# Queries and keys transposed once instead of doubled, in a one-core attention and recurrence kernel

## The chip, the cores and the metric

The kernel runs on one core of a Trainium2 chip. The metric is the device time in microseconds of one launch, as the median of several runs. Shorter is better.

## What is computed

One layer of a hybrid encoder for a prompt of 2048 frames and a running stream of 64 frames with 128 cached ones. The model width is 1024. There are four attention heads (two maps with a query and key width of 64, values of 128) and four recurrent heads with a 128x128 state. Cut to what matters:

```python
qa, ka, va, za, qr, fr, ir, zr = _project(_rmsnorm(h, norm_g), w_in)
q = qa.reshape(b, s, ATTN_HEADS, 2, ATTN_HEAD_DIM)       # two maps of 64
k = ka.reshape(b, s, ATTN_HEADS, 2, ATTN_HEAD_DIM)
scores = einsum('bqhmd,bkhmd->bhmqk', q, k) * ATTN_SCALE + bias   # -inf where not visible
p = softmax(scores)
a = p[:, :, 0] - lam * p[:, :, 1]
oa = einsum('bhqk,bkhe->bqhe', a, v)
h_new, orec = _rec_scan(silu(qr), key(fr), log_f(fr), ir)   # chunkwise, 64 frames
y = _rmsnorm(h + concat(_rmsnorm(oa) * silu(za), _rmsnorm(orec) * silu(zr)) @ w_out, final_g)
```

The outputs are y, the new keys and values, and the recurrent states, for the prompt and for the sample.

## The kernel before, in words

**Tiles and stages.** The rows are cut into 17 tiles of 128 rows: t=0 to 15 are the prompt, t=16 is the sample (`SAMPLE`). The outer loop runs over the four heads h=0 to 3, the inner one over the 17 tiles. Head 0 also normalises and transposes the rows of x, and keeps them in memory for the others. After the last head an epilogue multiplies the merged heads with `w_out` (L751).

**Every engine has its order written out by hand**, one function `head` for each engine, and semaphores tie the engines together. On TensorE (PE), `project(h, t)` (L532 to L576) multiplies tile t with the weights of head h, in 16 steps: half b=1 (the recurrent columns) and then half b=0 (attention), eight steps `kt` each, three matmuls of 128x512 a step (L562). Work of the tile before is put between the steps: the q·k products `qk` (L679 to L689, matmul L687) from kt=2 of b=1 on, the recurrent scores (L588) at kt=2 of b=0, and the transposes of the recurrence (L657 to L659) at kt=6. In head 0 the eight transposes of x (L526) come at kt=2 of b=1, just before the first q·k. Then `attend(h, t-1)` (L607 to L649) transposes the weights of the tile before (L625), does the recurrent output (L601 to L604), the transposes of queries and keys of tile t (`transpose_qk`, L661 to L674), and last the products with the values (L634) of the last chunk of keys. A chunk has up to four blocks of 128 keys.

**Splitting into two parts.** fp32 products are made from two float32r parts, a high one (a rounded copy) and a low one (the rest). For q·k the contraction of 64 is doubled: the operand `kp[:, m]` of map m holds the high part of its keys in 64 partitions and the low part in the other 64, and the query operand `q2[:, m, part]` holds the same query part in both halves. Two accumulating matmuls (part 0 and part 1) give the score.

**From the projection to q·k.** This is the chain that the change touches:

1. ScalarE (ACT), `attention_columns` (L833 to L847): L836 copies queries and keys of both maps out of `pab`, each of the four pieces of 64 columns written twice side by side, into `qn` (128x512). After the first copy of transposed weights (`at`, L873) it copies the keys once more into `kn` (L841), from where they go out to memory.
2. PE, `transpose_qk`: four transposes of 128x128 (L666) give all four pieces doubled in the partitions, in the PSUM buffer `tb`. At t=16 two more for the cached keys `kc` (L673).
3. ACT, `copy_qk` (L888 to L901): the high parts, `q2` (L892, 128x256) and `kp` (L894, 128x256).
4. VectorE (DVE), `split_qk` (L1097 to L1106): the low parts, `q2` (L1101, 128x256) and, on partitions 64 to 127 alone, `kp` (L1094 in `low_keys`, 64x256). This sends the signal `t_evac`.
5. PE waits for `t_evac` (L682) before the first q·k of the tile, three steps into the next projection. In head 0 the x transposes wait for the same signal (L522).

VectorE then turns each q·k product into biased scores (L1148). GpSimd (POOL) computes the exponents of the recurrence (L1370 to L1376), and with VectorE the low parts of the next head's weights (`w_lo`, L1303 and L1025) in tile t=16.

Of the kernel before, what the change touches and what calls it, by code (L numbers as in the profile page):

```python
# [25 lines left out]
P = 128  # L26
# [5 lines left out]
HD = 64  # L32
# [7 lines left out]
CACHE_SLOT = PT  # L40
# [62 lines left out]
def build(nc, x_prompt, x_sample, cache_k, cache_v, state_h, norm_g, w_in, lambda_qk, subln_g, rec_lb,  # L103
# [5 lines left out]
    with ctx:  # L109
# [19 lines left out]
        at = sb("at", [P, 2, 512])  # L129
        qn = sb("qn", [P, 4, P])  # L130
        q2 = sb("q2", [P, 2, 2, P], f32r)
# [36 lines left out]
        def raw_piece(weights, b, kt):  # L168
# [7 lines left out]
        xn = vv[:, 0:2 * KT, :].rearrange("p (a k) c -> p a (k c)", a=2)  # L176
        kc = sb("kc", [P, 2, P])
        ident = sb("ident", [P, P])
# [39 lines left out]
            k_out0=16 * EVEN, k_out1=16 * ODD, v_out=16 * NT, mix_out0=16 * EVEN, mix_out1=16 * ODD,  # L218
            h_out=16, hs_out=16, cache_in=64, **LO_PER)
        PRIME = dict(a_evac=1, pb_free=1, fin_done=1, qk_free=2, t_evac=2, gates=1,  # L220
# [75 lines left out]
        def _(sp):  # L296
# [73 lines left out]
            def head(h, last):  # L370
# [23 lines left out]
                for t in range(NT):  # L394
# [11 lines left out]
                    if t == 3:  # L406
# [4 lines left out]
                        else:  # L411
# [4 lines left out]
                            need(sp, h - 1, "qk_t", NT + 1)  # L416
                        for d in range(2):
                            sp.dma_start(kc[:, :, HD * d:HD * d + HD],
                                         one_head(cache_k[0, 0]).rearrange("t (m e) -> t m e", m=2)
                                         ).then_inc(S["cache_in"], 16)  # L420
                        sp.dma_start(vv[:, CACHE_SLOT, :], one_head(cache_v[0, 0])).then_inc(S["cache_in"], 16)
# [90 lines left out]
        def _(pe):  # L512
# [81 lines left out]
            def rec_output(h, t):  # L594
# [3 lines left out]
                if t == SAMPLE:  # L598
                    need(pe, h, "cache_in", 64)
                s_in = state if t < PT else state_s  # L600
# [6 lines left out]
            def attend(h, t, first, following):  # L607
                if t == SAMPLE:
                    need(pe, h, "cache_in", 64)
                need(pe, h, "fin_done", t)  # L610
# [50 lines left out]
            def transpose_qk(h, t):  # L661
                u = t_use["qk", t]
                need(pe, h, "t_evac", u - 1)
                need(pe, h, "qk_nat", t + 1)
                for j in range(4):
                    last = tr(tb[:, u % 2, P * j:P * j + P], qn[:, j, :], ident[:, :])  # L666
                last.then_inc(S["qk_t"], 1)
                if t == SAMPLE:
                    u = t_use["cache", t]
                    need(pe, h, "t_evac", u - 1)  # L670
                    need(pe, h, "cache_in", 64)
                    for m in range(2):
                        last = tr(tb[:, u % 2, P * m:P * m + P], kc[:, m, :], ident[:, :])  # L673
                    last.then_inc(S["qk_t"], 1)  # L674

# [99 lines left out]
        def _(act):  # L775
# [57 lines left out]
            def attention_columns(h, t, weights):  # L833
                need(act, h, "proj_done", t + 1)
                pa = pab[:, 0, :]
                F(qn[:, :, :].rearrange("p j (d e) -> p j d e", d=2),  # L836
                  pa[:, 0:2 * P].rearrange("p (j e) -> p j e", j=4).unsqueeze(2).to_broadcast([P, 4, 2, HD]),
                  ACT.Copy).then_inc(S["qk_nat"], 1)
                weights(0)
                need(act, h, f"k_out{t % 2}", 16 * (t // 2))  # L840
                F(kn[:, t % 2, :], pa[:, P:2 * P], ACT.Copy)  # L841
                if t == 0:
# [38 lines left out]
            def copy_recurrence(h, t):  # L881
# [4 lines left out]
                F(kt_[:, :], tb[:, u % 2, 2 * P:3 * P], ACT.Copy, scale=lbh[:, 1:2]).then_inc(S["t_evac"], 1)  # L886

            def copy_qk(h, t):  # L888

                u = t_use["qk", t]  # L890
                need(act, h, "qk_t", t + 1)
                F(q2[:, :, 0, :], tb[:, u % 2, 0:2 * P].rearrange("p (m c) -> p m c", m=2), ACT.Copy)  # L892
                s0 = slot_of(t) * P
                F(kp[:, :, s0:s0 + P], tb[:, u % 2, 2 * P:4 * P].rearrange("p (m c) -> p m c", m=2), ACT.Copy  # L894
                  ).then_inc(S["qk_hi"], 1)
                if t == SAMPLE:
                    u = t_use["cache", t]
                    need(act, h, "qk_t", NT + 1)
                    s0 = CACHE_SLOT * P
                    F(kp[:, :, s0:s0 + P], tb[:, u % 2, 0:2 * P].rearrange("p (m c) -> p m c", m=2), ACT.Copy  # L900
                      ).then_inc(S["qk_hi"], 1)  # L901

# [95 lines left out]
        def _(dve):  # L998
# [28 lines left out]

            v.memset(ones[:, :], 1.0)
            dve.wait_ge(S["gains_in"], 16)
# [61 lines left out]
            def low_keys(u, col, s0):  # L1091

                keys = kp[HD:P, :, s0:s0 + P]
                tt(keys, tb[HD:P, u % 2, col:col + 2 * P].rearrange("p (m c) -> p m c", m=2), keys.bitcast(f32),  # L1094
                   ALU.subtract).then_inc(S["t_evac"], 1)

            def split_qk(h, t):  # L1097

                u = t_use["qk", t]
                need(dve, h, "qk_hi", t + 1)  # L1100
                tt(q2[:, :, 1, :], tb[:, u % 2, 0:2 * P].rearrange("p (m c) -> p m c", m=2),  # L1101
                   q2[:, :, 0, :].bitcast(f32), ALU.subtract)
                low_keys(u, 2 * P, slot_of(t) * P)
                if t == SAMPLE:
                    need(dve, h, "qk_hi", NT + 1)
                    low_keys(t_use["cache", t], 0, CACHE_SLOT * P)  # L1106
# [323 lines left out]
```

## Time and profile before

| | us |
|---|---|
| median of 3 runs | 1550.55 |
| the three runs | 1547.85, 1550.55, 1550.83 |
| the profiled execution | 1548.09 |
| its span, first to last instruction | 1546.3 |
| PE busy in the span | 1501.3 (97%) |
| VectorE busy | 928.3 (60%) |
| ScalarE busy | 858.5 (56%) |
| GpSimd busy | 694.3 (45%) |

The span is part of the profiled execution's own time. A recorded matmul overlaps the next one, so the busy time of PE is not a sum of the durations. In the rows "out<-in" are the names of the program's tensors, "PEld" is PE's weight load, and a value in brackets is idle time before the instruction with what ended it.

### The profile page before, as it was taken

What the parts mean: (1) busy time and instruction counts of PE and PEld (TensorE: products, weight loads), DVE (VectorE), ACT (ScalarE), POOL (GpSimd) and SP (SyncE); (2) the same over time, 40 slices, a digit from 0 to 9 for tenths busy, and PEclk for the clock granted to TensorE, in tenths of its full rate; (3) what the DMA queues carried; (4) which work ended last, traced back from release to release, by engine and by line L of the source; (5) the groups of instructions that cost most, each with busy time, mean ns of one, the idle gap of its engine ahead of it and who ended that gap; (6) DMA issues with size and microseconds to landing.
All of it is one profiled execution on the core that took longest, in us unless ns stands there. A gap on an engine that the chain in (4) does not pass through costs nothing.

```text
span 1546.3 us, 25546 instructions
## 1 busy us (share of the span) xinstructions
PE 1501.3 (97%) x8432; PEld 1285.3 (83%) x8432; DVE 928.3 (60%) x2078; ACT 858.5 (56%) x2326; POOL 694.3 (45%) x1417
## 2 busy tenths in 40 slices
PE   5999999998999999989999999989999999999997
PEld 4888888887888888878888888878888888788886
DVE  6676666767555666684565666766556665732332
ACT  5566666676556555665555555855555556521121
POOL 6665555447554444365544444475444434400000
PEclk8999999999999999999999999999999999999999
DMA  8235222241542221124342221214322210234332
GB/s 229 91 117 170 93 82 79 89 146 52 153 128 94 69 69 42 65 65 121 102 135 69 68 70 49 79 51 158 126 72 70 69 66 24 94 130 149 133 122 68
DMA packets 99432, 149.13 MB, mean 96 GB/s; under 512 B 10288, under 2 KB 79792, under 8 KB 90608
## 3 DMA queue, kind: packets, MB, share of 16 engines
q1 hardware_dynamic: 99312, 147.62, 29.5%
q8 instruction: 64, 1.05, 0.3%
q14 instruction: 56, 0.46, 0.1%
HBM read 103.03 MB, written 44.56 MB: 95 GB/s over the span
## 4 chain that ended last, share of the span: by engine, by line
PE 85%; DVE 6%; POOL 4%; issue 2%; ACT 2%; DMA 0%; DVEq 0%; POOLq 0%; ACTq 0%
PE pab L562 42%; PE oar L634 7%; PE qkb L687 7%; PE qkb L751 6%; PE pab L751 6%; PE qkb L588 5%; PE tb L625 3%; DVE scores L1148 2%; PE tb L666 2%; ACT scores L907 1%; PE tb L526 1%; POOL w_lo L1303 1%; PE oar L604 1%; PE oar L601 1%; PE oar L603 1%
## 5 line engine op out<-in xcount | busy, mean ns | idle before, releaser
L562 PE MATMUL pab<-w_hi,xr 128*128 128x512 f32 x2176 | 785.1, 403 | 12.7 <-POOL w_lo L1303 8.5
L562 PEld LDWEIGHTS pab<-w_hi,xr 128*128 128x128 f32 x2176 | 413.0, 190 | 94.5 <-issue 14.4
L562 PE MATMUL pab<-w_lo,xr 128*128 128x512 f32 x1088 | 427.9, 393 | 0.0
L1370 POOL TENSOR_TENSOR dd<-dd 128x64 f32<-128x64 f32 x340 | 121.4, 357 | 485.9 <-DVE dd L1131 485.9
L562 PEld LDWEIGHTS pab<-w_lo,xr 128*128 128x128 f32 x1088 | 207.4, 191 | 33.0
L687 PE MATMUL qkb<-kp,q 128*128 128x512 f32 (+3 forms) x656 | 185.3, 364 | 3.0 <-DVE mxs L1148 2.8
L1148 DVE CUSTOM_DVE_ANT_0 scores<-qkb,bias 128x512 f32<-128x512 f32 (+4 forms) x136 | 84.8, 625 | 146.8 <-PE qkb L687 146.7
L907 ACT ACTIVATE scores<-scores,nmx 128x128 f32<-128x128 f32 (+16 forms) x136 | 156.9, 1163 | 17.0 <-DVE nmx L1158 17.0
L852 ACT ACTIVATE fb<-pab 128x256 f32<-128x256 f32 x68 | 26.1, 384 | 245.2 <-PE pab L562 245.2
L1101 DVE TENSOR_TENSOR q<-tb,q 128x256 fp32r<-128x256 f32 x68 | 28.8, 424 | 208.0 <-ACT kp L894 207.9
L634 PE MATMUL oar<-vv,at 128*128 128x128 f32 x1104 | 151.4, 276 | 0.1
L687 PEld LDWEIGHTS qkb<-kp,q 128*128 128x128 f32 x656 | 119.4, 188 | 34.4 <-DVE mxs L1148 12.0
L1349 POOL TENSOR_TENSOR kq<-qt,xx 128x896 f32<-128x896 f32 x68 | 144.4, 2124 | 1.3 <-ACT xx L916 1.3
L634 PEld LDWEIGHTS oar<-vv,at 128*128 128x128 f32 x1104 | 136.5, 192 | 1.7 <-ACT at L873 0.3
L1292 POOL TENSOR_SCALAR tms<-tsq 128x1 f32<-128x1 f32 x34 | 7.9, 233 | 278.2 <-ACT w_raw L786 103.0
L1148 DVE CUSTOM_DVE_ANT_0 scores<-qkb,bias,mxs 128x512 f32<-128x512 f32 (+2 forms) x192 | 121.3, 646 | 11.4 <-DVE mxs L1148 6.5
L588 PEld LDWEIGHTS qkb<-kq 128*128 128x128 f32 x816 | 100.7, 191 | 12.4 <-issue 4.7
L1088 DVE TENSOR_REDUCE st<-masked 128x128 f32<-128x768 f32 x68 | 105.1, 1546 | 2.3
L588 PE MATMUL qkb<-kq 128*128 128x128 f32 x816 | 103.0, 276 | 3.5 <-issue 2.9
L1371 POOL TENSOR_TENSOR dd<-dd 128x64 f32<-128x64 f32 x340 | 103.9, 306 | 0.0
L1171 DVE SCALAR_TENSOR_TENSOR scores<-scores,cneg 128x512 f32<-128x512 f32 (+4 forms) x164 | 101.6, 668 | 2.4
L873 ACT ACTIVATE at<-tb 128x512 f32<-128x512 f32 (+3 forms) x164 | 88.7, 541 | 23.6 <-PE tb L625 23.6
(152 smaller groups left out, 2637.5 us busy)
## 6 DMA issues: line engine op xcount, KB each, us to landing
xr<-xs SPq DMA_DIRECT2D x51, 1024.0 KB, 5.2
xs<-xr SPq DMA_DIRECT2D x17, 1024.0 KB, 3.9
w_raw<-in_w_in SPq DMA_DIRECT2D x48, 256.0 KB, 5.9
mix<-mx SPq DMA_DIRECT2D x68, 128.0 KB, 2.1
xr<-mix SPq DMA_DIRECT2D x17, 512.0 KB, 5.2
w_raw<-in_x_prompt SPq DMA_DIRECT2D x16, 512.0 KB, 4.0
scores<-in_x_prompt SPq DMA_DIRECT2D x16, 512.0 KB, 4.5
out<-vv SPq DMA_DIRECT2D x16, 512.0 KB, 3.0
```

The costliest lines, as they stand in the source:

```text
L562: last = mm(pab[:, b, :], x, w[:, kt, 512 * b:512 * b + 512], start=(kt == 0 and part == 0 and w is w_hi), stop=(kt == KT - 1 and part == 1))
L588: last = mm(qkb[:, u % 2, P * j:P * j + P], kl[:, b, :], ql[:, q, :], start=True, stop=True)
L634: last = mm(oar[:, 0, 0:VD], at[0:n, u % 2, b:b + P], vv[0:n, slot, :], start=(c == 0 and j == 0), stop=(c == len(chunks) - 1 and j == len ...
L687: last = mm(qkb[:, u % 2, 0:w], q2[:, m, part, :], kp[:, m, k0:k0 + w], start=(part == 0), stop=(part == 1))
L751: last = mm(bank[:, b, :], x, w[:, kt, 512 * b:512 * b + 512], start=(kt == 0 and part == 0 and w is w_hi), stop=(kt == KT - 1 and part == 1))
L907: last = F(scores[:, m, 0:n], scores[:, m, 0:n], ACT.Exp, bias=nmx[:, m:m + 1], scale=SCALE, accum_out=sums[:, m:m + 1])
L1088: v.tensor_reduce(st[:, :], masked[:, :, :].rearrange("p l c -> p c l"), AX.X, ALU.add).then_inc(S["rec_acc"], 1)
L1148: v.tensor_tensor_reduce(out=scores[:, m, off:off + w], in0=qkb[:, u % 2, 0:w], in1=bias[:, zero + off:zero + off + w], scale=1.0, scalar= ...
L1171: stt(scores[:, 0, off:off + w], scores[:, 1, off:off + w], cneg[:, 0:1], scores[:, 0, off:off + w], ALU.mult, ALU.add).then_inc(S["combin ...
L1349: g.tensor_tensor(ql[:, :, :], qt[:, :].unsqueeze(1).to_broadcast([P, NS, P]), xx[:, NX - NS:NX, :], ALU.mult).then_inc(S["q_decayed"], 1)
L1370: g.tensor_tensor(o[:, :, 0, :], ref, c[:, :, 0, :], sub)
L1371: g.tensor_tensor(o[:, :, 1, :], c[:, :, 1, :], ref, sub)
```

## The change

Queries and keys are transposed once, as 128x128 with both maps side by side. `qn` shrinks to 128x128, and `kn` is transposed itself, so it is copied right after `qn` and ahead of the first copy of weights. After the transposes map m lies in partitions 64m to 64m+63 alone. Copies to and from the two halves build the doubled operands. `q2`'s high part is written to both halves for each map (four copies of 64x128), the high keys stay in their own half (two copies), and the low keys go into the other half. The low query part is now in its own half only, and the other half is zeroed once at the start. The order of halves in `kp` is thus mirrored for map 1, and the product of the two low parts is left out of the score. The cached keys come in one DMA and one transpose. `cache_in` now counts to 48.

```diff
@@ kernel buffers
-        qn = sb("qn", [P, 4, P])
+        qn = sb("qn", [P, P])
-        kc = sb("kc", [P, 2, P])
+        kc = sb("kc", [P, P])
@@ sync engine, at t == 3
-                        for d in range(2):
-                            sp.dma_start(kc[:, :, HD * d:HD * d + HD],
-                                         one_head(cache_k[0, 0]).rearrange("t (m e) -> t m e", m=2)
-                                         ).then_inc(S["cache_in"], 16)
+                        sp.dma_start(kc[:, :], one_head(cache_k[0, 0])).then_inc(S["cache_in"], 16)
@@ transpose_qk
-                for j in range(4):
-                    last = tr(tb[:, u % 2, P * j:P * j + P], qn[:, j, :], ident[:, :])
-                last.then_inc(S["qk_t"], 1)
+                tr(tb[:, u % 2, 0:P], qn[:, :], ident[:, :])
+                tr(tb[:, u % 2, P:2 * P], kn[:, t % 2, :], ident[:, :]).then_inc(S["qk_t"], 1)
...
-                    for m in range(2):
-                        last = tr(tb[:, u % 2, P * m:P * m + P], kc[:, m, :], ident[:, :])
-                    last.then_inc(S["qk_t"], 1)
+                    tr(tb[:, u % 2, 0:P], kc[:, :], ident[:, :]).then_inc(S["qk_t"], 1)
@@ attention_columns
-                F(qn[:, :, :].rearrange("p j (d e) -> p j d e", d=2),
-                  pa[:, 0:2 * P].rearrange("p (j e) -> p j e", j=4).unsqueeze(2).to_broadcast([P, 4, 2, HD]),
-                  ACT.Copy).then_inc(S["qk_nat"], 1)
+                need(act, h, f"k_out{t % 2}", 16 * (t // 2))
+                F(qn[:, :], pa[:, 0:P], ACT.Copy)
+                F(kn[:, t % 2, :], pa[:, P:2 * P], ACT.Copy).then_inc(S["qk_nat"], 1)
                 weights(0)
-                need(act, h, f"k_out{t % 2}", 16 * (t // 2))
-                F(kn[:, t % 2, :], pa[:, P:2 * P], ACT.Copy)
@@ copy_qk
+            def high_keys(u, col, s0):
+
+                for m in range(2):
+                    rows = slice(HD * m, HD * m + HD)
+                    last = F(kp[rows, m, s0:s0 + P], tb[rows, u % 2, col:col + P], ACT.Copy)
+                last.then_inc(S["qk_hi"], 1)
...
-                F(q2[:, :, 0, :], tb[:, u % 2, 0:2 * P].rearrange("p (m c) -> p m c", m=2), ACT.Copy)
-                s0 = slot_of(t) * P
-                F(kp[:, :, s0:s0 + P], tb[:, u % 2, 2 * P:4 * P].rearrange("p (m c) -> p m c", m=2), ACT.Copy
-                  ).then_inc(S["qk_hi"], 1)
+                for m in range(2):
+                    rows = slice(HD * m, HD * m + HD)
+                    for place in range(2):
+                        F(q2[HD * place:HD * place + HD, m, 0, :], tb[rows, u % 2, 0:P], ACT.Copy)
+                high_keys(u, P, slot_of(t) * P)
@@ vector engine, start
-            v.memset(ones[:, :], 1.0)
+            setup_link(v.memset(ones[:, :], 1.0))
+            for m in range(2):
+                rows = slice(HD - HD * m, P - HD * m)
+                tt(q2[rows, m, 1, :], ones[rows, :], ones[rows, :], ALU.subtract)
@@ low_keys and split_qk
-                keys = kp[HD:P, :, s0:s0 + P]
-                tt(keys, tb[HD:P, u % 2, col:col + 2 * P].rearrange("p (m c) -> p m c", m=2), keys.bitcast(f32),
-                   ALU.subtract).then_inc(S["t_evac"], 1)
+                for m in range(2):
+                    rows, place = slice(HD * m, HD * m + HD), slice(HD - HD * m, P - HD * m)
+                    last = tt(kp[place, m, s0:s0 + P], tb[rows, u % 2, col:col + P],
+                              kp[rows, m, s0:s0 + P].bitcast(f32), ALU.subtract)
+                last.then_inc(S["t_evac"], 1)
...
-                tt(q2[:, :, 1, :], tb[:, u % 2, 0:2 * P].rearrange("p (m c) -> p m c", m=2),
-                   q2[:, :, 0, :].bitcast(f32), ALU.subtract)
-                low_keys(u, 2 * P, slot_of(t) * P)
+                for m in range(2):
+                    rows = slice(HD * m, HD * m + HD)
+                    tt(q2[rows, m, 1, :], tb[rows, u % 2, 0:P], q2[rows, m, 0, :].bitcast(f32), ALU.subtract)
+                low_keys(u, P, slot_of(t) * P)
```

The order of ScalarE from the columns of the attention to the sums of squares, in a tile of head 0 with one chunk (`q` is the program's `q2`). Before:

```order
L836 ACTIVATE qn<-pab 128x512
L873 ACTIVATE at<-tb 128x256
L841 ACTIVATE kn<-pab 128x128
L844 ACTIVATE vv<-pab 128x128
L846 ACTIVATE zz<-pab 128x128
L847 ACTIVATE ez<-pab 128x128
L892 ACTIVATE q<-tb 128x2x128
L894 ACTIVATE kp<-tb 128x2x128
L878 ACTIVATE junk,ssq<-oar,rsum 128x128
```

And with the change, whose lines have other numbers:

```order
L831 ACTIVATE qn<-pab 128x128
L832 ACTIVATE kn<-pab 128x128
L865 ACTIVATE at<-tb 128x256
L836 ACTIVATE vv<-pab 128x128
L838 ACTIVATE zz<-pab 128x128
L839 ACTIVATE ez<-pab 128x128
L894 ACTIVATE q<-tb 64x128 x4
L884 ACTIVATE kp<-tb 64x128 x2
L870 ACTIVATE junk,ssq<-oar,rsum 128x128
```

`kn` has moved ahead of `at`, and six copies on 64 partitions stand in place of two on 128, ahead of the squares.

The order of VectorE around the low parts, in head 0, from the scan of the recurrence to the first biased scores. Before:

```order
L1131 SCALAR_TENSOR_TENSOR dd<-ones,lf 128x128
L1012 SCALAR_TENSOR_TENSOR w_raw<-w_raw,trs 128x1024
L1101 TENSOR_TENSOR q<-tb,q 128x2x128
L1094 TENSOR_TENSOR kp<-tb,kp 64x2x128
L1148 ISA scores,mxs<-qkb,bias 128x512
```

With the change:

```order
L1134 SCALAR_TENSOR_TENSOR dd<-ones,lf 128x128
L1009 SCALAR_TENSOR_TENSOR w_raw<-w_raw,trs 128x1024
L1105 TENSOR_TENSOR q<-tb,q 64x128 x2
L1095 TENSOR_TENSOR kp<-tb,kp 64x128 x2
L1151 ISA scores,mxs<-qkb,bias 128x512
```

Four subtractions on 64 partitions stand in place of two; nothing has changed its place.

## Rows read from the trace of the kernel before

**Rows 1.** The page: busy time of each engine, and the granted clock in 40 slices.
```profile
PE 1501.3 (97%) x8432; PEld 1285.3 (83%) x8432; DVE 928.3 (60%) x2078; ACT 858.5 (56%) x2326; POOL 694.3 (45%) x1417
...
PEclk8999999999999999999999999999999999999999
```

**Rows 2.** Waits of PE over the whole span: total us, times, longest.
```profile
PE pab L562 <- POOL w_lo L1303: 8.5, 3, 2.8
...
PE tb L666 <- ACT qn L836: 1.7, 5, 0.8
```

**Rows 3.** Chain of waits, head 2: start us, us, what.
```profile
713.16 0.11 PE tb L658
...
762.18 0.44 PE tb L666 x4
```

**Rows 4.** Timeline where head 2 begins: start us, us, engine, line, [idle before].
```profile
692.76 0.68 PE L562 MATMUL pab<-w_hi,xr 128*128 128x512 f32 x1 [2.83 <-POOL w_lo L1303]
```

**Rows 5.** Timeline of head 2, t=1, from the attention columns to q·k.
```profile
714.81 0.60 ACT L836 ACTIVATE qn<-pab 128x512 f32<-128x512 f32 x1 [0.51 <-PE pab L562]
...
715.30 0.27 ACT L873 ACTIVATE at<-tb 128x128 f32<-128x128 f32 x1
...
715.55 0.63 PE L666 MATMUL tb<-ident,qn 128*128 128x128 f32 x4 [0.22 <-ACT qn L836]
715.61 0.30 ACT L844 ACTIVATE vv<-pab 128x128 f32<-128x128 f32 x1
715.77 0.31 ACT L846 ACTIVATE zz<-pab 128x128 f32<-128x128 f32 x1
715.91 0.30 PEld L634 LDWEIGHTS oar<-vv,at 128*128 128x128 f32 x2
...
716.01 0.39 PE L634 MATMUL oar<-vv,at 128*128 128x128 f32 x2
...
716.21 0.39 ACT L892 ACTIVATE q<-tb 128x256 fp32r<-128x256 f32 x1
...
716.49 0.38 ACT L894 ACTIVATE kp<-tb 128x256 fp32r<-128x256 f32 x1
...
716.90 0.42 DVE L1101 TENSOR_TENSOR q<-tb,q 128x256 fp32r<-128x256 f32 x1 [2.15 <-ACT kp L894]
...
717.34 0.43 DVE L1094 TENSOR_TENSOR kp<-tb,kp 64x256 fp32r<-64x256 f32 x1
...
718.09 0.42 PEld L687 LDWEIGHTS qkb<-kp,q 128*128 128x128 f32 x2
718.32 0.40 PE L687 MATMUL qkb<-kp,q 128*128 128x256 f32 x2
```

**Rows 6.** Groups of instructions: busy us, mean ns of one, idle before.
```profile
L1111 DVE TENSOR_TENSOR nb<-pab,rc 128x128 f32<-128x128 f32 x68 | 19.2, 283 | 0.0
```

**Rows 7.** Timeline of head 1, t=16: two L1094 in a row.
```profile
680.01 0.77 DVE L1094 TENSOR_TENSOR kp<-tb,kp 64x256 fp32r<-64x256 f32 x2
```

**Rows 8.** Timeline of head 2, t=6, 7 and 8: L1094 and the first q·k load.
```profile
798.73 0.43 DVE L1094 TENSOR_TENSOR kp<-tb,kp 64x256 fp32r<-64x256 f32 x1
...
799.70 0.42 PEld L687 LDWEIGHTS qkb<-kp,q 128*128 128x128 f32 x2
...
816.34 0.43 DVE L1094 TENSOR_TENSOR kp<-tb,kp 64x256 fp32r<-64x256 f32 x1
...
817.54 0.42 PEld L687 LDWEIGHTS qkb<-kp,q 128*128 128x128 f32 x2
...
834.46 0.43 DVE L1094 TENSOR_TENSOR kp<-tb,kp 64x256 fp32r<-64x256 f32 x1
...
835.85 0.41 PEld L687 LDWEIGHTS qkb<-kp,q 128*128 128x128 f32 x2
```

**Rows 9.** Timeline of head 0, t=1: L1094 and the first x transpose.
```profile
56.50 0.43 DVE L1094 TENSOR_TENSOR kp<-tb,kp 64x256 fp32r<-64x256 f32 x1
...
57.25 1.03 PEld L526 LDWEIGHTS tb<-ident,w_raw 128*128 128x128 f32 x8
```

More of the change, by code:

```diff
@@ L218, in build @@
             k_out0=16 * EVEN, k_out1=16 * ODD, v_out=16 * NT, mix_out0=16 * EVEN, mix_out1=16 * ODD,
-            h_out=16, hs_out=16, cache_in=64, **LO_PER)
+            h_out=16, hs_out=16, cache_in=48, **LO_PER)
         PRIME = dict(a_evac=1, pb_free=1, fin_done=1, qk_free=2, t_evac=2, gates=1,
@@ L598, in rec_output @@
                 if t == SAMPLE:
-                    need(pe, h, "cache_in", 64)
+                    need(pe, h, "cache_in", 48)
                 s_in = state if t < PT else state_s
@@ L608, in attend @@
                 if t == SAMPLE:
-                    need(pe, h, "cache_in", 64)
+                    need(pe, h, "cache_in", 48)
                 need(pe, h, "fin_done", t)
@@ L670, in transpose_qk @@
                     need(pe, h, "t_evac", u - 1)
-                    need(pe, h, "cache_in", 64)
-                    for m in range(2):
-                        last = tr(tb[:, u % 2, P * m:P * m + P], kc[:, m, :], ident[:, :])
-                    last.then_inc(S["qk_t"], 1)
+                    need(pe, h, "cache_in", 48)
+                    tr(tb[:, u % 2, 0:P], kc[:, :], ident[:, :]).then_inc(S["qk_t"], 1)
             def qk_units(t):
@@ L891, in copy_qk @@
                 need(act, h, "qk_t", t + 1)
-                F(q2[:, :, 0, :], tb[:, u % 2, 0:2 * P].rearrange("p (m c) -> p m c", m=2), ACT.Copy)
-                s0 = slot_of(t) * P
-                F(kp[:, :, s0:s0 + P], tb[:, u % 2, 2 * P:4 * P].rearrange("p (m c) -> p m c", m=2), ACT.Copy
-                  ).then_inc(S["qk_hi"], 1)
+                for m in range(2):
[3 more added lines that the diff above has]
+                high_keys(u, P, slot_of(t) * P)
                 if t == SAMPLE:
-                    u = t_use["cache", t]
                     need(act, h, "qk_t", NT + 1)
-                    s0 = CACHE_SLOT * P
-                    F(kp[:, :, s0:s0 + P], tb[:, u % 2, 0:2 * P].rearrange("p (m c) -> p m c", m=2), ACT.Copy
-                      ).then_inc(S["qk_hi"], 1)
+                    high_keys(t_use["cache", t], 0, CACHE_SLOT * P)
             def softmax_exp(h, t):
```

## The prediction

> **What bounds the kernel now.** I read the page first, then the list of what the TensorE waited for, then the chain of waits, and last the timeline of single tiles. The page shows the PE busy for 97% of the span at nearly the full granted clock (2.4 GHz) [rows 1]. The list of PE waits is short: its longest entry is 8.5 us in 3 waits, for GpSimd's `w_lo` pieces where one head ends and the next begins, and the wait of the transposes for the ScalarE copy `qn` is 1.7 us in 5 waits [rows 2]. So the bound is the PE's own order of instructions, and anything taken out of it inside a head moves the end, as long as no new wait appears. A new wait is the question here, because the change shortens the PE's part and lengthens the two engines that stand between the transposes and the q·k matmuls.
>
> **What comes out of the PE.** In the chain of waits a transpose costs 0.11 us: one alone has 0.11, four in a row have 0.44 [rows 3]. Their recorded length of 0.27 overlaps, so it is the spacing that counts. The change drops two of four in each of 68 tiles (17 tiles in 4 heads), and one of two for the cache in each sample tile.
> - Tiles that count: not t=16. After it the PE stands for 2.83 us for GpSimd's `w_lo` [rows 4]; a PE that arrives earlier only waits longer. That holds for all its four transposes' savings and the cache's. Not t=0 of head 0 either, whose transposes lie in the start-up. That leaves 63 tiles x 2 x 0.11 = 13.9 us.
> - At t=1 of each head the transposes wait for ScalarE's copy, 714.81 + 0.60 = 715.41 [rows 5]. Now they wait for two copies of 128 columns, which start 0.16 apart and last 0.30 (L844 to L846 in the same rows): 714.81 + 0.16 + 0.30 = 715.27, which is 0.14 earlier, x 4 heads = 0.6 us.
> - Gain: 14.5 us.
>
> **What goes into the chain behind the transposes.** Set the clock to zero at the first transpose of head 2, t=1 (715.55) [rows 5]. Before: the PE goes on to its next work (L634) at 0.46; ScalarE starts L892 at 0.66, L894 follows 0.28 later; VectorE starts at 1.35 and L1094 ends at 2.22. The keys are thus ready 1.76 after the PE went on. The first q·k weight load comes at 718.09, 0.32 after the keys.
> After the change, step by step:
> - Two transposes fewer: the PE goes on at 0.24, ScalarE starts at 0.44.
> - ScalarE: six copies of 64x128 in place of two of 128x256. No row has a copy on 64 partitions or one that changes partitions. The nearest rows are the 128-column copies L844 and L846, 0.16 apart; that is the low end. The high end is each copy waiting for the one before to finish, 0.31 apart (0.29 long, 0.02 between). I take 0.16, by the nearest rows on this engine: the last starts at 0.44 + 5 x 0.16 = 1.24 and ends at 1.53.
> - VectorE starts 0.03 later (as 716.90 follows 716.87), at 1.56, with four subtractions of 64x128 in place of two. A 128-column subtraction out of PSUM lasts 0.28 [rows 6]; with the 256-column one less 128 columns I take 0.29. What counts is the spacing. L1101 starts at partition 0, L1094 at 64, and they are 0.44 apart, 0.02 more than L1101's 0.42 [rows 5]. Two L1094 behind one another, both at 64, take 0.77 together, so they are only 0.34 apart [rows 7]. A change of half thus costs the overlap of 0.09 and 0.02. In the new order each of the three steps changes the half of an input or of the output, so I take 0.31: 4 x 0.29 + 3 x 0.02 = 1.22, and the keys are ready at 2.78.
> The Trainium skill's page "VectorE: DVE Perf Modes", section "Two Vector instructions with no wait between them", says that such an instruction is held until every earlier one has finished when an operand's start quadrant differs from the last one's. The trace agrees, with the 0.44 against 0.34. Without that rule the spacing would be 0.20, the keys would be ready 0.33 earlier, and the sum would be that of the third case below.
>
> The keys are now ready 2.78 - 0.24 = 2.54 after the PE goes on, 0.78 later than before. How much of it is covered is read tile by tile, as the time from L1094's end to the first q·k load. It depends on how many blocks of values the PE still multiplies between (the last chunk of the tile before): one block 0.32 (t=1, 5, 9, 13; [rows 5]), two blocks 0.54 (t=2, 6, 10, 14), three 0.77 (t=3, 7, 11, 15), four 0.96 (t=4, 8, 12; t=0 is about the same) [rows 8]. Head 0 is no better off: its x transposes (L526) sit before q·k and wait for the same signal, 57.25 against 56.93, again 0.32 [rows 9]. To this comes 0.07 of hidden slack: a q·k load stands 0.23 before its matmul but needs only 0.10 (L634 in the same rows), less some 0.05 for the signal [rows 5].
> - One block: 0.78 - 0.39 = 0.39, x 16 tiles = 6.2 us.
> - Two blocks: 0.78 - 0.61 = 0.17, x 16 = 2.7 us. Three and four blocks: nothing.
> - Head 0, t=0: VectorE's four operations last 0.35 longer than the two, and the PE waits for them there: 0.3 us.
> - Loss: 9.2 us, a wait of PE L687 (in head 0, L526) for VectorE's `kp`, which does not exist now.
>
> What costs nothing: on ScalarE the smaller `qn` copy gives back 0.33 (0.49 to 0.16 from start to start) and the later copies add 0.41, on an engine that idles 44% of the span [rows 1]. The cache DMA becomes one instead of two, and lands a dozen tiles before its use. The wait for the `kn` store now stands before `qn`, but that store is two tiles old. The zeroing at the start lies before the first input has arrived. The multiplications L687 have the same shapes as before.
>
> **Sum.** 14.5 - 9.2 = 5.3 us less. Against the profiled execution (1548.09 us; span 1546.3) that is 1542.8; its time stands 2.5 below the median of the runs shown, 1550.55, and so I forecast 1545.3 for a median.
> Own range of this case: 0.1 us on the chain's length is worth 3.2 to 4 us of the total, and I trust the chain to 0.15, so 1539 to 1552.
>
> **Rivals.**
> 1. *ScalarE is held too, and the kernel becomes slower.* Five of the six copies read or write another half than the one before. If ScalarE loses its overlap there as VectorE does, the copies are 0.31 apart instead of 0.16, the chain is 5 x 0.15 = 0.75 longer, and the keys come 1.53 late. Stalls: 1.14 x 16 + 0.92 x 16 + 0.69 x 16 + 0.50 x 16 = 52 us; less 14.5, plus 0.3, that is 38 more: 1588. For it: the only engine on which the trace shows a change of half does lose its overlap. Against it: it is another engine, all of whose operations start at partition 0 so far, so no row tells. It decides early: with keys 0.91 late, 0.13 more than I take, the stalls already eat the whole gain.
> 2. *No hold anywhere.* VectorE's four at 0.20 apart: the keys come 0.45 late, the one-block tiles stall 0.06 each, 1 us in all, and 13.2 us are won: 1537. For it: ordinary neighbours overlap by about 0.09 on VectorE. Against it: the 0.44 against 0.34 [rows 5, 7].
> 3. *The gain goes elsewhere.* The freed PE time could be absorbed where heads change, as it is at t=16 [rows 4], or the stalls could just balance it, 1550. Against it: the chain of waits runs over PE all through a head, and what leads into the change of head starts from the PE's last q·k.
>
> **How the numbers follow.** Forecast 0.5, ScalarE held 0.35, no hold 0.1, nothing 0.05. A measurement of this kernel can tell about 0.2% (3 us) from no change. Of the forecast's half three quarters lie beyond that on the fast side; with the no-hold case that is 0.47 faster. 0.12 is within, 0.41 slower (the rival, and the forecast's upper edge). The two signs hold nearly equal chances, so the range reaches into both: 1537 at the low end, the no-hold case; 1590 at the high end, the held case with little over it.
>
> **What would show it.** Transposes in tb at half their count, still 0.11 apart. ScalarE's `q` and `kp` copies 0.16 apart (forecast) or 0.31 (rival 1). VectorE's four subtractions 0.31 apart (or 0.20, rival 2). A new entry in the list of PE waits, q·k for `kp`, of about 0.4 in one-block tiles and 0.2 in two-block tiles, 9 us in all; or over 50 in all four kinds. The forecast is wrong if that entry is missing, or if it appears in three- and four-block tiles.

## The result and the profile after

The changed kernel takes 1574.61 us (median of 4 runs, 1570.88 to 1577.11), against 1549.95 for the kernel before in its 4 runs: the ratio is 1.0158, with a 95% interval of 1.0138 to 1.0178. It is slower by 24.7 us. The forecast was 1545.3 us, the rival "ScalarE is held too" 1588. The profiled execution of the changed kernel took 1577.11 us, with a span of 1575.4, 29.0 more than the span before, before rounding. It is 2.5 above the median of its runs, and the profiled one before stood 1.9 below the median of its four, so the traces show 29.0 where the medians differ by 24.7.

The page first: the busy times and the clock [rows 1].

```profile
span 1575.4 us, 25748 instructions
...
PE 1506.6 (96%) x8292; PEld 1269.4 (81%) x8292; DVE 939.2 (60%) x2220; ACT 908.9 (58%) x2602; POOL 693.4 (44%) x1417
...
PEclk9999999999999999999999999999999999999999
```

Nothing stands out in it. The PE is nearly as busy as before (96% against 97% of the span), because the recorded lengths of its matmuls overlap and hide small gaps. The other engines that compute are busy for 44% to 60% of the span. The next view does tell: what the PE waited for, first its matmuls, then its weight loads (columns: waited for, us in total, times, longest us).

```profile
PE qkb L681 <- DVE kp L1095: 17.8, 37, 0.7
```
```profile
PEld qkb L681 <- DVE kp L1095: 39.4, 49, 1.2
```

The entry that did not exist before [rows 2] is there, q·k waiting for VectorE's keys. The two lists differ by a factor of two for one and the same wait. The matmul list leaves out whatever the modelled end of the matmul before still covers; the list of the weight loads has close to the full time for which the PE's order stood still. A tile shows why the keys are late. This is head 2, t=1, the same place as [rows 5]:

```profile
730.44 0.30 PE L662 MATMUL tb<-ident,qn 128*128 128x128 f32 x1
730.57 0.27 PE L663 MATMUL tb<-ident,kn 128*128 128x128 f32 x1
730.68 0.39 PE L631 MATMUL oar<-vv,at 128*128 128x128 f32 x2
...
730.88 1.12 ACT L894 ACTIVATE q<-tb 64x128 fp32r<-64x128 f32 x4
...
732.01 0.55 ACT L884 ACTIVATE kp<-tb 64x128 fp32r<-64x128 f32 x2
...
732.60 0.59 DVE L1105 TENSOR_TENSOR q<-tb,q 64x128 fp32r<-64x128 f32 x2 [2.80 <-ACT kp L884]
...
733.21 0.59 DVE L1095 TENSOR_TENSOR kp<-tb,kp 64x128 fp32r<-64x128 f32 x2
...
733.85 0.30 PEld L681 LDWEIGHTS qkb<-kp,q 128*128 128x128 f32 x2 [1.13 <-DVE kp L1095]
```

Put zero at 730.44. The PE goes on at 0.24 and ScalarE starts at 0.44, both as predicted. ScalarE's six copies then take until 2.12: 1.68 for six of 0.27 to 0.28, one behind the other with no overlap, 0.28 apart. VectorE starts at 2.16, its four subtractions take 1.20, and the keys are ready at 3.36. That is 3.12 after the PE went on, against 1.76 before: 1.36 late, where the forecast had 0.78 and the rival 1.53.

**Where the time went.** I take the first transpose of each tile as its mark, and compare the distance from mark to mark in both traces. The stall of tile t lies between its mark and the next. Mean change of that distance, by the number of blocks that cover the chain:

```
blocks, tiles                              change   + 0.22 saved = stall   1.36 - cover, as the prediction has it
one   (t=1, 5, 9, 13), 16 tiles            +0.65        0.87               1.36 - 0.39 = 0.97
two   (t=2, 6, 10, 14), 16 tiles           +0.51        0.73               1.36 - 0.61 = 0.75
three (t=3, 7, 11, 15), 16 tiles           +0.34        0.56               1.36 - 0.84 = 0.52
four  (t=4, 8, 12), 12 tiles               +0.11        0.33               1.36 - 1.03 = 0.33
```

These tiles add 10.3 + 8.1 + 5.5 + 1.4 = 25.3 us. The three tiles t=0 of the later heads and the three changes of head add nothing in sum (at t=0 a stall of 0.4 takes back the 0.4 that the shorter transposes and the earlier copies save), the first tile of head 0 adds 1.6 (more on it below), and from the last t=16 on it is 2.6; the first mark comes 0.5 earlier, which goes off. That makes the 29.0. The 2.6 at the end are mostly the first matmuls of the epilogue: they waited 1.1 for VectorE's `kp` before, and now wait 3.0. At t=16 the cached keys' copies and subtractions come on top.

The mean of the three-block row hides one thing. At t=3, 7 and 11 the change is +0.32 in the mean, near the +0.30 that a stall of 0.52 gives. At t=15 it is +0.75 in heads 0 to 2 and -0.64 in head 3. There the last q·k products wait until VectorE has read an earlier score: in head 1 the first of these waits grows from 0.32 to 0.74 us, in head 3 it shrinks from 1.59 to 0.71. VectorE's product `kq`, which comes ahead of those scores, lasts 1.57 us in head 1, t=15, against 1.15 before. Why it lasts longer no run shows.

### The profile page after: what moved, and what is told of

Same layout as the page of the kernel before. It is cut to its first block, busy times and chain, and to the rows that moved or that the text cites. A ratio compares the mean times of both kernels' runs of the same rounds, so it can differ in the third digit from the quotient of the medians.

```text
span 1575.4 us, 25748 instructions
## 1 busy us (share of the span) xinstructions
PE 1506.6 (96%) x8292; PEld 1269.4 (81%) x8292; DVE 939.2 (60%) x2220; ACT 908.9 (58%) x2602; POOL 693.4 (44%) x1417
## 4 chain that ended last, share of the span: by engine, by line
PE 78%; DVE 9%; ACT 6%; issue 4%; POOL 3%; DMA 0%; DVEq 0%; POOLq 0%; SPq 0%; ACTq 0%
PE pab L559 37%; PE qkb L681 8%; PE oar L631 6%; PE qkb L745 6%; PE pab L745 6%; PE qkb L585 5%; PE tb L622 3%; ACT q L894 2%; DVE scores L1151 2%; DVE kp L1095 2%; DVE q L1105 2%; ACT kp L884 2%; PE tb L523 1%; PE tb L732 1%; PE pab L720 1%
## 5 line engine op out<-in xcount | busy, mean ns | idle before, releaser
L559 PEld LDWEIGHTS pab<-w_lo,xr 128*128 128x128 f32 x1088 | 207.6, 191 | 33.1
L681 PE MATMUL qkb<-kp,q 128*128 128x512 f32 (+3 forms) x656 | 191.3, 373 | 21.5 <-DVE kp L1095 17.8
L1105 DVE TENSOR_TENSOR q<-tb,q 64x128 fp32r<-64x128 f32 x136 | 39.2, 289 | 263.0 <-ACT kp L884 262.0
L681 PEld LDWEIGHTS qkb<-kp,q 128*128 128x128 f32 x656 | 116.2, 189 | 70.5 <-DVE kp L1095 39.4
L844 ACT ACTIVATE fb<-pab 128x256 f32<-128x256 f32 x68 | 26.1, 384 | 245.8 <-PE pab L559 245.8
```

What stands on the lines that cost most here:

```text
L559: last = mm(pab[:, b, :], x, w[:, kt, 512 * b:512 * b + 512], start=(kt == 0 and part == 0 and w is w_hi), stop=(kt == KT - 1 and part == 1))
L681: last = mm(qkb[:, u % 2, 0:w], q2[:, m, part, :], kp[:, m, k0:k0 + w], start=(part == 0), stop=(part == 1))
```

## Experiments

Each kernel differs from the changed one by the edit shown, except where it says otherwise.

**The transposes alone.** The kernel before, with two transposes instead of four and nothing else of the change. ScalarE and VectorE keep the number and sizes of their operations, and read the same transposed columns twice, so map 1's own queries and keys are left out.

```diff
-                for j in range(4):
-                    last = tr(tb[:, u % 2, P * j:P * j + P], qn[:, j, :], ident[:, :])
+                for j in range(2):
+                    last = tr(tb[:, u % 2, P * j:P * j + P], qn[:, 2 * j, :], ident[:, :])
```

> The kernel before with two transposes a tile instead of four, and nothing else: ScalarE and VectorE read the same transposed columns twice, with the same numbers and sizes of operations, so map 1 computes with map 0's queries and keys. Theory (the gain is as forecast and the loss is a wait): 14 to 15 us less than before, about 1535.5, transposes 0.11 us apart, no PE wait of q.k for the keys. Rival (the freed PE time never reaches the end, so the change had nothing to win): 1549 to 1551.

Measured: 1538.07 us, ratio 0.9926 (0.9909 to 0.9942). That is 2.6 us above the 1535.5 expected. From mark to mark, tiles from t=5 on are shorter by 0.22 (0.19 to 0.24), so 0.11 for a transpose holds to the hundredth. Tiles t=1 to 4 of heads 1 to 3 gain only 0.00 to 0.12. The keys do not hold them, as head 2, t=1, shows (timeline, then the wait of the PE's weight loads up to the first transpose of t=2):

```profile
711.40 0.41 PE L666 MATMUL tb<-ident,qn 128*128 128x128 f32 x2 [0.22 <-ACT qn L835]
...
713.13 0.43 DVE L1093 TENSOR_TENSOR kp<-tb,kp 64x256 fp32r<-64x256 f32 x1
...
713.72 0.42 PEld L686 LDWEIGHTS qkb<-kp,q 128*128 128x128 f32 x2
```
```profile
PEld qkb L588 <- DVE kq L1177: 0.6, 1, 0.6
```

The keys are ready at 2.16, and the first q·k load comes at 2.32 without a wait, 0.22 sooner than before. The gain is lost later, where the recurrent scores wait for VectorE's `kq`: 0.6 us instead of 0.4 at t=1, and 0.2 instead of nothing at t=2. At t=3 and 4 the first load for the products with the values comes 0.23 after the mark, 0.05 after ScalarE's copy `at` has ended; before it came at 0.33, so only 0.10 is gained. A faster PE has less cover for every wait, not only for the one that was looked at. The rest of the shortfall lies outside these tiles in this execution, 1.2 us in head 0's first tile and 1.4 at the changes of head.

**ScalarE without a change of half.**

```diff
-                    rows = slice(HD * m, HD * m + HD)
-                    for place in range(2):
-                        F(q2[HD * place:HD * place + HD, m, 0, :], tb[rows, u % 2, 0:P], ACT.Copy)
+                    for target in (q2[:, m, 0, :], spare[:, m, :]):
+                        F(target, tb[:, u % 2, 0:P], ACT.Copy)
```

The key copies change in the same way. This leaves out the separation of the two maps, so the scores are not the right ones.

> The changed kernel with all six ScalarE copies behind the transposes starting at partition 0, on 128 partitions, the second copy of the queries into a buffer nobody reads; attention is computed with unsplit halves. Theory (a copy that changes the half it reads or writes loses its overlap): copies 0.16 us apart instead of 0.28, keys ready 0.6 us earlier, 26 to 32 us less than the changed kernel, 1543 to 1549. Rival (six copies cost 0.28 each by their number, or because they read PSUM and write float32r): as the changed kernel, 1572 to 1577.

Measured: 1541.49 us, ratio 0.9954 (0.9938 to 0.9971), 1.5 below the expected range. Timeline, head 2, t=1:

```profile
728.46 0.30 ACT L893 ACTIVATE q<-tb 128x128 fp32r<-128x128 f32 x1
728.63 0.29 ACT L893 ACTIVATE spare<-tb 128x128 fp32r<-128x128 f32 x1
728.79 0.31 ACT L893 ACTIVATE q<-tb 128x128 fp32r<-128x128 f32 x1
728.94 0.32 ACT L893 ACTIVATE spare<-tb 128x128 fp32r<-128x128 f32 x1
729.10 0.50 ACT L884 ACTIVATE kp<-tb 128x128 fp32r<-128x128 f32 x2
...
729.63 0.59 DVE L1104 TENSOR_TENSOR q<-tb,q 64x128 fp32r<-64x128 f32 x2 [2.33 <-ACT kp L884]
```

The six copies are now 0.16 to 0.17 apart, though each has twice the partitions. This kernel is the prediction's likeliest case made real: ScalarE at 0.16, VectorE held. From mark to mark it measures +0.16 with one block, -0.04 with two, -0.22 with three and with four; the prediction's terms give 0.39 - 0.22 = +0.17, 0.17 - 0.22 = -0.05, and -0.22.

**VectorE without a change of half.**

```diff
-                    last = tt(kp[place, m, s0:s0 + P], tb[rows, u % 2, col:col + P],
-                              kp[rows, m, s0:s0 + P].bitcast(f32), ALU.subtract)
+                    last = tt(kp[:, m, s0:s0 + P], tb[:, u % 2, col:col + P],
+                              q2[:, m, 0, :].bitcast(f32), ALU.subtract)
```

> The changed kernel with all four VectorE subtractions starting at partition 0, on 128 partitions; the low parts of the keys are computed from the wrong operand. ScalarE is as in the changed kernel. Theory (VectorE too loses its overlap at each change of half): the four are 0.20 us apart instead of 0.30, keys ready 0.3 us earlier in every tile, 16 to 21 us less than the changed kernel, about 1556. Rival (0.30 is what a 128-column subtraction out of PSUM takes): no change, 1572 to 1577.

Measured: 1554.05 us, ratio 1.0029 (1.0018 to 1.0040).

```profile
721.13 0.49 DVE L1103 TENSOR_TENSOR q<-tb,q 128x128 fp32r<-128x128 f32 x2 [2.81 <-ACT kp L884]
721.53 0.48 DVE L1094 TENSOR_TENSOR kp<-tb,q 128x128 fp32r<-128x128 f32 x2
```

(Timeline, head 2, t=1.) Two take 0.49 instead of 0.59, and the pairs follow each other at 0.40: 0.20 apart instead of 0.30. The edit leaves out the right low parts of the keys.

**Both engines without a change of half.** The two edits together, with what both leave out.

> Both engines without a change of half: the change's six copies on ScalarE and its four subtractions on VectorE all start at partition 0 and cover 128 partitions (the second copies of the queries go into a spare buffer, the low keys are computed from a wrong operand, so the attention is computed on other operands than the reference's). The theory (each engine loses its overlap at a change of half, and the chain behind the transposes is the sum of both): copies 0.16 apart, subtractions 0.20 apart, keys ready at 0.44 + 5 x 0.16 + 0.29 + 0.03 + 3 x 0.20 + 0.29 = 2.45 after the first transpose; no wait of the PE for the keys is left beyond some hundredths, and the time is that of the prediction's case without holds, 1537, at most 1539. The rival (the two losses don't add: once ScalarE is free, VectorE's hold costs nothing): it stays at the 1541.5 that the copies alone gave.

Measured: 1536.07 us, ratio 0.9909 (0.9893 to 0.9924). With the other three this makes a square:

```
                        VectorE changes halves     VectorE does not
ScalarE changes halves        1574.6                    1554.1
ScalarE does not              1541.5                    1536.1
```

ScalarE's holds cost 33.1 us, or 18.0 once VectorE is free of its own; VectorE's cost 20.5, or 5.4 once ScalarE is free. The losses are not simply added, since a stall only begins where the cover ends. The rival of this run is refuted: VectorE's holds still cost 5.4.

**Which change of half is it?** The same six copies in another order, so that each step changes only what is read, only what is written, or nothing.

```diff
+                    if m == 0:
+                        F(q2[rows, m, 0, :], tb[rows, u % 2, 0:P], ACT.Copy)
+                        F(kp[rows, m, s0:s0 + P], tb[rows, u % 2, P:2 * P], ACT.Copy)
+                        F(q2[other, m, 0, :], tb[rows, u % 2, 0:P], ACT.Copy)
...
```

The second half follows with `q2` to its own place, `kp`, and `q2` into the other half.

> The changed kernel with the six ScalarE copies in another order, so that they change half three times instead of five: reads 0,0,0,64,64,64 and writes 0,0,64,64,64,0. Theory (each change of the half read or written costs the overlap): two spacings fall from 0.28 to 0.16 us, the second and the fifth, keys ready 0.24 us earlier, about 15 us less than the changed kernel, 1558 to 1562. Rival one (only a change of the half written counts): a third spacing, before the fourth copy, falls too, 0.36 us earlier, about 1551. Rival two (the number of copies counts alone): 1572 to 1577.

Measured: 1557.72 us, ratio 1.0055 (1.0038 to 1.0072).

```profile
735.88 0.27 ACT L895 ACTIVATE q<-tb 64x128 fp32r<-64x128 f32 x1
736.05 0.26 ACT L896 ACTIVATE kp<-tb 64x128 fp32r<-64x128 f32 x1
736.32 0.27 ACT L897 ACTIVATE q<-tb 64x128 fp32r<-64x128 f32 x1
736.60 0.27 ACT L899 ACTIVATE q<-tb 64x128 fp32r<-64x128 f32 x1
736.78 0.26 ACT L900 ACTIVATE kp<-tb 64x128 fp32r<-64x128 f32 x1
737.05 0.28 ACT L901 ACTIVATE q<-tb 64x128 fp32r<-64x128 f32 x1
```

(Timeline, head 2, t=1.) Steps with the same halves are 0.17 and 0.18 (L895 to L896, L899 to L900). L896 to L897 changes only the half written, 0.27; L897 to L899 only the half read, 0.28; L900 to L901 only the half written, 0.27. Either change by itself costs the full overlap, and both together (0.28 in the changed kernel) cost no more than one. Reordering alone thus wins 16.9 us of the changed kernel's loss, at no cost.

**The cross copies beside VectorE.** Full result. ScalarE first copies each half to its own place and signals. The copies into the other half are made from SBUF while VectorE subtracts, under a signal of their own that q·k waits for.

```diff
-                    for place in range(2):
-                        F(q2[HD * place:HD * place + HD, m, 0, :], tb[rows, u % 2, 0:P], ACT.Copy)
-                high_keys(u, P, slot_of(t) * P)
+                    F(q2[rows, m, 0, :], tb[rows, u % 2, 0:P], ACT.Copy)
+                    last = F(kp[rows, m, s0:s0 + P], tb[rows, u % 2, P:2 * P], ACT.Copy)
+                last.then_inc(S["qk_hi"], 1)
...
+                    last = F(q2[other, m, 0, :], q2[rows, m, 0, :].bitcast(f32), ACT.Copy)
+                last.then_inc(S["q_cross"], 1)
```

> The whole result is computed. ScalarE first makes the four copies that stay in their own half, grouped by half (one change), then signals VectorE; the two copies of the queries into the other half are read from SBUF and run beside VectorE, and the first q.k waits for them too. Theory (the loss is the length of the chain between transposes and keys, and the price is per change of half): four copies take 0.90 us instead of 1.68, keys ready 0.78 earlier, stalls left only in one-block tiles at about 0.2 us, 3 us in all above the two-transposes kernel, 1541: faster than both kernels. Rival (the loss is ScalarE's work, which is as large as before): about 1570. A second risk: the cross copies finish after VectorE; then q.k waits for ScalarE.

Measured: 1536.77 us, ratio 0.9922 (0.9909 to 0.9935): faster than the kernel before and the changed one, and level with the version that has no change of half at all. It is also 4 us below the 1541 expected. The stalls left in one-block tiles came as expected, 2.6 us more than with the transposes alone; what is better than there lies at the changes of head (3.5 us) and before the first mark (1.4), and no run tells the cause. Timeline, head 2, t=1 (first transpose at 709.58):

```profile
710.03 0.27 ACT L895 ACTIVATE q<-tb 64x128 fp32r<-64x128 f32 x1
...
710.65 0.26 ACT L896 ACTIVATE kp<-tb 64x128 fp32r<-64x128 f32 x1
...
710.95 0.63 ACT L901 ACTIVATE q<-q 64x128 fp32r<-64x128 f32 x2
710.95 0.59 DVE L1112 TENSOR_TENSOR q<-tb,q 64x128 fp32r<-64x128 f32 x2 [2.00 <-ACT kp L896]
...
711.55 0.59 DVE L1102 TENSOR_TENSOR kp<-tb,kp 64x128 fp32r<-64x128 f32 x2
```

ScalarE and VectorE start the second stage at the same time, and the keys are ready at 2.56 instead of 3.36. VectorE's subtractions are still held, and tiles with one block still pay: their distance from mark to mark is about as before the change (-0.02 in the mean), and not 0.22 shorter. Tiles t=15 of heads 0 to 2 are 0.60 longer than before: VectorE's `kq` lasts 2.0 us there, and in head 1 the last q·k products wait 1.15 until VectorE has read an earlier score.

**q·k one step later.** The changed kernel, with the q·k units of each tile, and head 0's x transposes, behind one more step of the projection.

```diff
-                after = 2 if t > 0 else 4
+                after = 3 if t > 0 else 4
```

> The changed kernel with the first q.k of each tile, and in head 0 the x transposes, put one step (0.68 us of matmuls) later in the projection; nothing else. Theory (the loss is uncovered waiting of the PE): stalls of 0.98, 0.76, 0.53 and 0.34 us fall to 0.30, 0.08, 0, 0, so 35 us of 42 come back, 1540 to 1544, unless the q.k of the tiles with eight units now crowd at the end and VectorE holds them, up to 8 us more. Rival (the loss is not a wait that later use covers): 1570 or more.

Measured: 1558.24 us, ratio 1.0055 (1.0042 to 1.0069), a miss by 14 us. The PE's weight loads wait 8.1 us for the keys, no longer 39.4, but two other waits grew:

```profile
PEld qkb L681 <- DVE mxs L1151: 22.4, 32, 1.4
PEld qkb L585 <- DVE kq L1181: 13.6, 35, 0.6
```

The first was 11.9 in the changed kernel, and the second was not there. To see them without the stalls for the keys, the same edit went on top of the version with the cross copies beside VectorE:

> Both edits, cross copies beside VectorE and q.k one step later; the whole result is computed. Theory: no PE wait for the keys at all, so 1538 as with two transposes alone, plus what the crowding of q.k costs in tiles 12 to 15 (0 to 8 us), which this run gives by itself. If it is slower than the run with the cross copies alone (1541), the crowding costs more than the 3 us of stalls.

Measured: 1551.34 us, ratio 1.0010 (1.0001 to 1.0019), so that the later step costs 14.6 us there. Mark to mark against the version without it, nearly no tile is shorter; t=3 is 0.42 longer, t=6 to 11 are 0.1 to 0.4 longer, and t=12, 13 and 14 are 0.5 to 0.7 longer each. The same two waits, without the later step and with it:

```profile
PEld qkb L682 <- DVE mxs L1158: 13.6, 32, 1.2
PEld qkb L585 <- DVE kq L1188: 4.4, 9, 0.8
```
```profile
PEld qkb L682 <- DVE mxs L1158: 21.8, 32, 1.2
PEld qkb L585 <- DVE kq L1188: 15.3, 32, 0.9
```

They grow by 8.2 and 10.9 us, and the 4.0 for the keys go, 15.1 in all. The larger part is the wait for `kq`. VectorE's order has the scores of q·k ahead of it: in head 1, t=3, the first scores start 4.46 us after the mark instead of 3.78, and `kq` starts at 7.80 instead of 7.09, so that the recurrent scores, which stay where they were in the PE's order, wait 0.55 for it. The other part is in tiles with eight q·k units. Timeline, head 1, t=12, the last units of its eight:

```profile
602.34 0.74 DVE L1158 CUSTOM_DVE_ANT_0 scores<-qkb,bias,mxs 128x512 f32<-128x512 f32 x1
602.47 0.30 PEld L682 LDWEIGHTS qkb<-kp,q 128*128 128x128 f32 x2 [0.93 <-DVE mxs L1158]
...
603.14 0.30 PEld L682 LDWEIGHTS qkb<-kp,q 128*128 128x128 f32 x2 [0.37 <-DVE mxs L1158]
```

There are no more steps behind which the last units could stand, so they pile up at the start of half b=0. There each has to wait until VectorE has read an earlier score (0.93 and 0.37; 0.25 and 0.37 in the version with the cross copies alone). The expectation had counted the stalls that go, and 8 us for what comes; the latter was much too low, and did not have the wait for `kq` at all. In this order the start of q·k can't be moved without moving VectorE's work behind it and the end of q·k.

**A signal for each half.** The version with the cross copies, where VectorE subtracts the first half while ScalarE copies the second. Full result.

```diff
-                last.then_inc(S["qk_hi"], 1)
+                    last.then_inc(S[("qk_half", "qk_hi")[m]], 1)
...
-                need(dve, h, "qk_hi", t + 1)
                 for m in range(2):
+                    need(dve, h, ("qk_half", "qk_hi")[m], t + 1)
```

> The version with the cross copies beside VectorE, and in it VectorE told of the first half's query and key copy by a signal of their own, so that it subtracts the first half while ScalarE copies the second. Full result. What the keys' time still costs in tiles with one block to cover is 0.2 to 0.3 (periods of t=5, 9, 13 are as before the change, and not 0.22 shorter). Theory (only the length of the chain counts): VectorE starts at about 0.92 after the first transpose instead of 1.37, four subtractions at 0.30, keys at about 2.12 instead of 2.56, 0.12 later against the PE than before the change, nearly covered: those tiles get their 0.22 back, t=1 and t=2 about 0.1, in all about 3 us, so 1533.5 (1532 to 1535). Rival (both engines reading the same PSUM bank at once, or the wait between VectorE's pairs, gives the time back): subtractions longer than 0.29 or the copies over 0.28 apart, and 1536 to 1538 as it was.

Measured: 1537.12 us, ratio 0.9919 (0.9905 to 0.9932), no different from the 1536.77 without it. The keys are ready when the theory said, at 2.11 (expected 2.12). The tiles t=5, 9 and 13 win back 0.09 to 0.23, 0.16 to 0.24 and 0.08 to 0.13, 2.0 us together; t=1 and 2, from which 0.1 each was expected, win nothing. The rival's number came (1536 to 1538), but not its mechanism: VectorE's subtractions last 0.28 to 0.30, as without the edit, and ScalarE's copies out of PSUM are as far apart as without it, within 0.02. The first tile of head 0 lasted 2.9 us longer in the trace, and so the sum is nil. Whether it lasts longer in every run is not known, since each kernel has one profiled execution.

## Why the prediction was wrong, point by point

**The reading of the bound was right.** The PE's order sets the end inside a head, the transposes are worth 0.11 each, and a new wait decides. The transposes alone gave 11.4 us between medians, of 13.9 forecast for them. What was missed is that at t=1 to 4 other waits, for `kq` and for `at`, take back up to all of the gain.

**The step that failed** is the term of ScalarE's copies: "The nearest rows are the 128-column copies L844 and L846, 0.16 apart; that is the low end. The high end is each copy waiting for the one before to finish, 0.31 apart (0.29 long, 0.02 between). I take 0.16, by the nearest rows on this engine". Its bounds held the truth, and the choice between them was wrong. The copies came 0.28 apart, because each step of the change's order reads or writes another half. L844 and L846 were near in engine and shape, but both start at partition 0, and the property that differed was the one that counted. For just that property the nearest rows were VectorE's, 0.44 against 0.34 [rows 5, 7]. The prediction used them for VectorE and set them aside for ScalarE. With 0.16 the kernel takes 1541.5, as the version without ScalarE's holds shows, against the 1545.3 forecast; there the tiles came as forecast, and the changes of head came out 2.6 us shorter than before in the trace, for which the prediction had no term. The prediction's own sign of being wrong came too: the wait for the keys stands in three- and four-block tiles.

**Rival 1 was the case that came**, and its size was off. It gave 1588, and 1574.6 was measured. It had taken copies of 0.29 with 0.02 between; they are 0.27 to 0.28 long with nothing between, which over five steps makes 0.15 of the 0.17 by which the lateness came out smaller (1.36 against 1.53). At 0.17 in each of 60 tiles that is some 10 us. Its second half was right too: all four kinds of tile stall.

**VectorE's term was right**: 0.31 forecast, 0.30 measured, and 0.20 without a change of half. The Trainium skill's page "VectorE: DVE Perf Modes", section "Two Vector instructions with no wait between them", speaks of Vector instructions alone; by its words ScalarE's copies could have gone either way. The case without holds was put at 1537; 1536.1 was measured. That this is so near is in part luck: the trace of that version is only 10.7 us shorter than the one before, where the medians differ by 14.2 and the case had 13.2.

**The cover, block by block, was right** to 0.04 for two, three and four blocks. With one block the stall was 0.10 smaller than lateness less cover, all of it in tiles t=1, which lost only 0.09 (head 0) to 0.42, where the others lost 0.68 to 0.83. In the trace of the kernel before, one more weight load waits in head 2, t=1, for VectorE's `kq`, 0.4 us; after the change this wait is gone, since q·k stands longer in front of it. A stall of 0.97 in place of one of 0.4, less 0.22 saved, makes +0.35, and +0.38 was measured there. The prediction had looked at the wait for the keys alone. The version with the cross copies pays at the same place the other way round, 0.3 for the keys and 0.6 for `kq`, which is why its tiles t=1 in heads 1 to 3 gain nothing:

```profile
PEld qkb L588 <- DVE kq L1178: 0.4, 1, 0.4
```
```profile
PEld qkb L585 <- DVE kq L1188: 0.6, 1, 0.6
PEld qkb L682 <- DVE kp L1102: 0.3, 1, 0.3
```

(The PE's weight loads in head 2 from the first transpose of t=1 to that of t=2, before the change, and in the version with the cross copies beside VectorE.)

**Terms were missing.** The epilogue's wait for `kp` grew from 1.1 to 3.0. At t=15 the last q·k products wait longer for VectorE in heads 0 to 2, 0.4 us each, and shorter in head 3, which nearly cancels. And the first tile of head 0, costed at 0.3, took 1.6 more in the profiled execution; 1.2 of that appears with the transposes alone, and nothing of it in the version without any change of half, whose chain is longer than before too. So it is mostly not the longer chain.

## What to carry to other kernels

When a wide operation is split into pieces that move between the halves of the partitions, price every step at full length, without overlap, on both ScalarE and VectorE, until a row shows otherwise. Order such pieces so that neighbours read and write the same halves, and put the ones that must cross beside another engine's work instead of in the chain. When the nearest row for a new operation is looked up, ask first which property is new, and take the row that shares that one, even from another engine. Where an engine's order gets shorter, look at every wait that follows in it, since each loses cover.

## What the hardware showed that was not expected

- **ScalarE loses its overlap at a change of half**, read or written. Copies of 64x128 or 128x128 out of PSUM follow each other at 0.16 to 0.18 while both start partitions stay, and at 0.27 to 0.28, their full length, when one changes. The overlap is thus about 0.11. Only starts 0 and 64 were tried. The Trainium skill's page "ScalarE: Activation LUTs", section "What ACT_TABLE_LOAD costs", has an overlap of about 93 ns for ACTIVATEs back to back. The 0.11 here is near it; the section has no case in which the overlap is lost.
- **The PE's clock at the start of the program differs from trace to trace**, and it can spend what a chain has won. Behind the first transposes of q and k the PE waits for VectorE's `kp`, and VectorE first does one operation of 2.3 us on the bias. Windows of the changed kernel, of the version with the cross copies, and of the one with a signal for each half (columns: window, its length, busy time of PE, PEld, DVE, ACT, POOL, granted clock, DMA share, GB/s):

```profile
38.00:42.00 4.00, 0.64 (x4) 0.67 (x5) 3.11 (x6) 0.00 (x0) 4.00 (x9) 0.93 0.33 122
42.00:46.00 4.00, 4.00 (x18) 3.54 (x17) 0.91 (x7) 2.91 (x4) 2.73 (x4) 0.64 0.02 4
```
```profile
38.00:42.00 4.00, 0.66 (x6) 0.69 (x7) 3.10 (x6) 0.00 (x0) 4.00 (x9) 1.00 0.20 80
42.00:46.00 4.00, 4.00 (x23) 3.44 (x22) 2.57 (x7) 2.92 (x4) 2.73 (x3) 1.00 0.02 6
```
```profile
38.00:42.00 4.00, 0.53 (x3) 0.56 (x4) 3.22 (x6) 0.00 (x0) 4.00 (x8) 0.76 0.11 44
42.00:46.00 4.00, 4.00 (x16) 3.61 (x15) 0.63 (x5) 2.92 (x4) 2.73 (x4) 0.50 0.02 4
```

  The PE stood idle for 3.42, 3.64 and 4.87 us. In the second case it went on at 2.4 GHz, and the next 4 us hold 23 records of matmuls; in the third at 1.2 GHz throughout (0.50), with 16; in the first it ran at the lower level for part of the time. Before the change the PE was granted 0.50 from 34 to 38 us, was still busy for 3.56 of the 4 us from 38 to 42, and was at 1.00 from 42 on. In the three traces above the first transpose of t=1 comes at 55.8, 54.3 and 56.9 us; these differences of 1 to 3 us are as much as some of the edits are worth. It can't be told from one profiled execution of each which of it belongs to a kernel.
